# Experts taken one of each group in turn, and the way from the output projection to them rebuilt

## The reference, cut to what matters

```python
x = x + gate1 * (jnp.concatenate([gm_out, ssm_out], axis=-1) @ w_out[l])
h = rmsnorm(x, norm2_g[l]) * (1 + scale2) + shift2
x = x + gate2 * hier_moe(h, ...)          # then one final rmsnorm

def hier_moe(t, ...):
    g_prob = softmax(t @ w_rg + b_rg)               # 4 groups, the best one is taken
    e_logits = (t @ w_re + b_re).reshape(-1, 4, 4)  # 4 experts in each, the best two of the group
    gates = ...                                     # 16 weights per token, two of them not zero
    hid = silu(t @ w_gate[e]) * (t @ w_up[e]) * gates[:, e]     # 2048 -> 512
    out = sum over e of hid @ w_down[e]                         # 512 -> 2048
```

## Time and profile before

| | |
|---|---|
| three runs | 1430.35 (median), 1426.56, 4198.51 us |
| the profiled execution | 1430.36 us, of which its span is 1428.3 us |
| PE busy | 1198.2 us (84%) |
| PEld, DVE, ACT, POOL busy | 643.5, 310.4, 200.8, 116.0 us |
| chain that ended last | PE 65%, DMA 26%, DVE 6%, issue 1%, ACT 1% |
| L1163 (full branch, gate and up) | x256, 64 for each of four experts |
| L1160 (few branch, gate and up) | x1536, 128 for each of twelve experts |
| DMA moved | 401.09 MB, 281 GB/s in the mean |

### The profile page before, as it was taken

How to read it: one execution, slowest core, us unless ns; L and a number is a source line. 1 busy time by engine, 2 the same in 40 slices (tenths; PEclk the granted TensorE clock), 3 DMA queues, 4 the chain that set the end, 5 groups by cost and what they waited for, 6 DMA issues and landing times.

```text
span 1428.3 us, 16027 instructions
## 1 busy us (share of the span) xinstructions
PE 1198.2 (84%) x6320; PEld 643.5 (45%) x6321; DVE 310.4 (22%) x623; ACT 200.8 (14%) x385; POOL 116.0 (8%) x129
## 2 busy tenths in 40 slices
PE   2678999999999999999992299999988788778740
PEld 0225565565545445545542244444544444444420
DVE  0101222131122224120018500111111211111128
ACT  2001111012021222100012100010111111111102
POOL 2010000000000002000005100000000000000016
PEclk8778999989999999999995599999999999999975
DMA  9997787737557529642530468877999999999953
GB/s 333 421 350 279 282 336 291 278 143 294 232 197 281 230 73 357 225 189 77 226 118 33 177 247 305 308 276 296 378 413 412 414 412 402 393 412 412 425 204 105
DMA packets 71717, 401.09 MB, mean 281 GB/s; under 512 B 6489, under 2 KB 6713, under 8 KB 39645
## 3 DMA queue, kind: packets, MB, share of 16 engines
q1 hardware_dynamic: 63216, 368.59, 66.0%
q0 software_dynamic: 6944, 23.99, 5.1%
q10 hardware_dynamic: 1520, 7.98, 1.4%
HBM read 394.85 MB, written 17.22 MB: 288 GB/s over the span
## 4 chain that ended last, share of the span: by engine, by line
PE 65%; DMA 26%; DVE 6%; issue 1%; ACT 1%; SPq 0%; POOLq 0%; DVEq 0%
DMA arena<-in_w_up_dram 20%; PE bank L817 20%; PE bank L896 10%; PE bank L1163 8%; PE bank L823 5%; DMA arena<-in_w_ada_dram 5%; PE bank L810 5%; PE bank L1160 5%; PE bank L1186 4%; PE bank L914 1%; PE bank L1183 1%; DMA arena<-expert_rows 1%; PE bank L840 1%; DVE arena L1480 1%; DVE arena L1481 1%
## 5 line engine op out<-in xcount | busy, mean ns | idle before, releaser
L817 PE MATMUL bank<-arena 128*128 128x512 f32 x640 | 286.0, 597 | 0.0
L1160 PE MATMUL bank<-arena 128*64 128x256 f32 x1536 | 185.8, 399 | 59.9 <-DMA arena<-in_w_gate_dram 32.6
L817 PEld LDWEIGHTS bank<-arena 128*128 128x128 f32 x640 | 117.9, 190 | 135.5 <-issue 134.4
L1160 PEld LDWEIGHTS bank<-arena 128*64 128x64 f32 x1536 | 112.5, 143 | 138.0 <-DMA arena<-in_w_gate_dram 44.8
L896 PE MATMUL bank<-arena 128*128 128x320 f32 x512 | 143.2, 440 | 3.8 <-DVE arena L1258 3.8
L810 PE MATMUL bank<-arena 128*32 128x512 f32 x768 | 101.4, 669 | 44.5 <-DMA arena<-in_w_ada_dram 32.7
L896 PEld LDWEIGHTS bank<-arena 128*128 128x128 f32 x512 | 97.9, 192 | 51.1 <-issue 7.8
L1163 PE MATMUL bank<-arena 128*128 128x512 f32 x256 | 113.5, 604 | 7.5 <-issue 7.5
L1183 PE MATMUL bank<-arena 128*64 128x512 f32 x384 | 85.0, 595 | 6.0 <-DVE arena L1629 6.0
L1626 DVE SCALAR_TENSOR_TENSOR arena<-bank,arena 128x512 f32<-128x512 f32 x16 | 12.0, 751 | 348.5 <-PE bank L1160 232.4
L1163 PEld LDWEIGHTS bank<-arena 128*128 128x128 f32 x256 | 49.5, 194 | 70.2 <-issue 70.2
(11 more groups left out here) (314 smaller groups left out, 856.8 us busy)
## 6 DMA issues: line engine op xcount, KB each, us to landing
arena<-in_w_ada_dram SPq DMA_DIRECT2D x48, 2048.0 KB, 14.9
arena<-in_w_gate_dram SPq DMA_DIRECT2D x32, 2048.0 KB, 26.3
arena<-in_w_up_dram SPq DMA_DIRECT2D x32, 2048.0 KB, 27.1
arena<-in_w_down_dram SPq DMA_DIRECT2D x32, 2048.0 KB, 26.2
arena<-in_w_in_dram SPq DMA_DIRECT2D x20, 2048.0 KB, 7.8
arena<-in_w_out_dram SPq DMA_DIRECT2D x8, 2048.0 KB, 8.8
arena<-mod_final POOLq DMA_DIRECT2D x6, 1024.0 KB, 11.8
arena<-expert_rows SPq DMA_DIRECT2D x8, 512.0 KB, 8.6
```

The lines of the kernel that those rows point to most:

```text
L817: last = mm(banks[j][:, :], lhsT=xT_[:, t, OFF[j]:OFF[j] + P], rhs=w, start=start, stop=stop)
L1160: last = mm(PB[bank][64 * h:64 * h + 64, 0:HALF], lhsT=XeT[:, t0 + t, 0:64], rhs=slots_w[slot][:, t, HALF * h:HALF * h + HALF], start=star ...
```

## The change

Three things change together.

First, the experts run one of each group in turn: place 4r + g of the order holds expert 4g + r. SP's loads follow nested loops over r and g, and the routing masks are written in the new order (`by_turn`), so every table behind them is in it too. 

Second, the norm rows keep their column order. The `by_t` permutation is gone, and the gate and up weights are loaded so that the four input rows of a piece lie together in each partition (8 KB pieces instead of 16 KB), as the down weights already were; the transposes of the gathered rows read every fourth column instead. DVE multiplies x1 with the scale in each quarter (`scaled`) and, once the factor is known, applies factor and shift with two instructions per tile (`shifted`); POOL's part of the norm and its clearing of Xe are gone, and ACT issues all stores, two per tile.

Third, the last quarter of the projection goes token tile by token tile, with a semaphore `outp_done` after each prompt tile, so that residual, squares, factor and rows of a tile follow while PE works on the next. The wait of a down weight load for `h2_stored[2]` falls away, and small buffers move to places that are cleared early.

```diff
             def expert(e, i):
-                    if isinstance(i, int) and s == W1:
-                        sp.wait_ge(h2_stored[2], 16)
-                        src = w[0, bass.ds(e, 1)].rearrange("e (p t) n -> p (e t) n", t=KT)[:, 8 * half:8 * half + 8, :]
-                        dst = slots_w[s]
+                        src = w[0, bass.ds(e, 1)].rearrange("e (a p b) n -> p (e a) (b n)", p=P, b=4)[:, 2 * half:2 * half + 2, :]
+                        dst = slots_four[s]
...
-            with sp.Fori(1, NE) as e:
-                expert(e, e)
+            with sp.Fori(1, 4) as g:
+                expert(4 * g, g)
+            with sp.Fori(1, 4) as r:
+                with sp.Fori(0, 4) as g:
+                    expert(4 * g + r, 4 * r + g)
...
-            pool.memset(arena[:, SA + 2048:MX], 0.0).then_inc(cleared, 1)
-            pool.tensor_tensor(o, o, by_t(a2b[0:DEC, 1, :]), ALU.mult).then_inc(h2_sample, 1)
-            pool.tensor_tensor(o, o, by_t(s2b[0:DEC, 1, :]), ALU.add).then_inc(h2_sample, 1)
-            pool.memset(Xe, 0.0).then_inc(cleared, 1)
+            pool.wait_ge(yT_out, 24)
+            for a, b in ((cT_off, cT_end), (cw_off, cw_end), (wdt_off, wdt_end)):
+                pool.memset(arena[:, a:b], 0.0).then_inc(cleared, 1)
...
+            def store_h2(j):
+                n = NT[j]
+                act.wait_ge(h2_ready, j + 1)
+                act.dma_start(h2_d[OFF[j]:OFF[j] + n, 0:ROW], h2_part[j][0][0:n]).then_inc(h2_stored[j], 16)
+                act.dma_start(h2_d[OFF[j]:OFF[j] + n, ROW:D], h2_part[j][1][0:n]).then_inc(h2_stored[j], 16)
...
+                x1_square(3, j)
+                act.wait_ge(var, j + 2)
+                act.activation(st[0:n, 20 + j:21 + j], st[0:n, 16 + j:17 + j], ACT.Sqrt).then_inc(std, 1)
+                x1T_copy(3, j)
+                if j < 2:
+                    store_h2(j)
             act.wait_ge(gexp_in, 1)
...
+            store_h2(2)
...
-                        last = tr(PB[2 + k][:, P * c:P * c + P], Xe[:, P * t:P * t + P], ident)
+                        a, b = 4 * P * (t // 4), t % 4
+                        last = tr(PB[2 + k][:, P * c:P * c + P], Xe[:, a + b:a + 4 * P:4], ident)
...
+            def scaled(q, j):
+                n, cols = NT[j], slice(N * q, N * q + N)
+                dst = h2_part[j][1][0:n] if q == 3 else h2_part[j][0][0:n, cols]
+                step(V.tensor_tensor(dst, x1[0:n, j, cols], a2b[0:n, STREAM[j], cols], ALU.mult))
...
+            def shifted(j):
+                n, b = NT[j], STREAM[j]
+                left, right = h2_part[j][0][0:n], h2_part[j][1][0:n]
+                V.scalar_tensor_tensor(left, left, col(24 + j, 1, n), s2b[0:n, b, 0:ROW], ALU.mult, ALU.add)
+                V.scalar_tensor_tensor(right, right, col(24 + j, 1, n), s2b[0:n, b, ROW:D], ALU.mult, ALU.add).then_inc(h2_ready, 1)
...
+            for j in range(2):
+                dve.wait_ge(outp_done, j + 1)
+                residual(3, j)
+                scaled(3, j)
+                rstd_of(j)
+                shifted(j)
+            dve.wait_ge(slot_used[W1], 16)
+            residual(3, 2)
+            scaled(3, 2)
+            rstd_of(2)
             dve.wait_ge(lgp, 12)
...
             payload(0)
+            shifted(2)
             dve.wait_ge(rankp, 1)
```

More of the change, by code:

```diff
@@ L195, in trunk @@
         rt = take(3, 8)
+        assert ptr[0] <= cT_end
+        ptr[0] = cw_off
+        pay = take(3, COLS, 4)
         rk = take(3, COLS)
@@ L753, in _ @@
-            act.wait_ge(var, 2)
-            act.activation(st[:, 6:9], st[:, 3:6], ACT.Sqrt).then_inc(std, 1)
-            act.wait_ge(slot_used[W1], 16)
-            act.wait_ge(rstd2, 1)
-            act.activation(by_t(h2p[2][0:DEC], out=True), by_t(x1[0:DEC, 2, :]), ACT.Copy, scale=st[0:DEC, 11:12]).then_inc(h2_sample, 1)
-            for j in range(2):
-                act.wait_ge(h2_ready, j + 1)
-                act.dma_start(h2_d[OFF[j]:OFF[j] + P, :], h2p[j]).then_inc(h2_stored[j], 16)
+            def store_h2(j):
[3 more added lines that the diff above has]
+                act.dma_start(h2_d[OFF[j]:OFF[j] + n, ROW:D], h2_part[j][1][0:n]).then_inc(h2_stored[j], 16)
@@ new lines, in _ @@
+            for q in range(3):
+                if q:
+                    for j in range(3):
+                        x1T_copy(q - 1, j)
+                for j in range(3):
+                    x1_square(q, j)
+            for j in range(3):
+                x1T_copy(2, j)
+            for j in range(3):
+                n = NT[j]
+                if j == 0:
+                    act.wait_ge(outp_read, 9)
+                x1_square(3, j)
[4 more added lines that the diff above has]
+                    store_h2(j)
@@ L1488, in _, with residual @@
             V.tensor_scalar(fold, iota, 63.5, -64.0, ALU.is_gt, ALU.mult)
-            step(V.memset(rk, -1.0))
+            V.memset(rk, -1.0)
             for k in range(3):
                 V.tensor_scalar(w4[:, k, :], iota[:, 0:4], -1.0, 4.0, ALU.mult, ALU.add)
+            def residual(q, j):
+                k, n = 3 * q + j, NT[j]
+                bank, cols = PB[4 * (q % 2) + j], slice(N * q, N * q + N)
+                if j < 2:
+                    last = V.tensor_tensor(tmp, bank[:, :], g1b[:, 0, cols], ALU.mult)
+                else:
+                    for h in range(2):
+                        r, c0 = slice(DEC * h, DEC * h + DEC), HALF * h
+                        last = V.tensor_tensor(tmp[0:n, c0:c0 + HALF], bank[r, 0:HALF], g1b[r, 1, N * q + c0:N * q + c0 + HALF], ALU.mult)
+                last.then_inc(outp_read, 1)
+                dve.wait_ge(outp_read, k + 1)
+                V.tensor_tensor(x1[0:n, j, cols], x1[0:n, j, cols], tmp[0:n], ALU.add).then_inc(x1_ready, 1)
+                dve.wait_ge(x1_ready, k + 1)
@@ new lines, in shifted @@
+            def shifted(j):
[3 more added lines that the diff above has]
+                V.scalar_tensor_tensor(right, right, col(24 + j, 1, n), s2b[0:n, b, ROW:D], ALU.mult, ALU.add).then_inc(h2_ready, 1)
+            dve.wait_ge(g1_in, 32)
+            dve.wait_ge(xr_in, 48)
+            for q, (slot, used) in enumerate(((A1, 21), (W1, 15), (A1, 22))):
+                dve.wait_ge(slot_used[slot], used)
+                for j in range(3):
+                    residual(q, j)
+                if q == 0:
+                    dve.wait_ge(s2_in, 64)
+                for j in range(3):
+                    scaled(q, j)
```

160 lines of the change are left out of this document (76 added, 84 removed).

## The result

The changed kernel takes **1374.8 us** in the median (1373.5 to 1376.2), the kernel before 1428.5 in the same comparison: a ratio of 0.961, 95% interval [0.958, 0.964]. The prediction was 1370 us with a range of 1354 to 1389. The ratio is of fast runs alone: one of the four of the kernel before, 4198.5 us, counts in its median and not in the ratio.

The account below looks back on a forecast made before the run. PE idles in the transition behind DVE's wide norm instructions; four full experts are PE bound, eleven DMA bound. 1428.3 - 34 - 27 + 0.5 = 1367.8 us of span, plus 2.1 around it: 1370 us, range 1354 to 1389.

Parts of the forecast that it names:

- the transition: From the projection's last matmul to the first expert's first: -27 us, bounds -21 and -28.
- -26.9 - 0.8 + 0.7 + 0.5: Up to the first expert's matmul: logits reduced earlier, POOL's clearing of Xe gone, `shifted(2)` before the ranks, strided transposes.
- the load layout: Gate and up weights in 8 KB pieces instead of 16 KB: taken as 0 us.
- Faster loads: Rival in the experts' stage: all loads run at 422 GB/s rather than 408, 15 us gained, 1355 us; chance 0.11.
- the order of the experts: Experts' stage: three later full experts cost 32.4 us instead of 44.7; -34 us, bounds 28 and 37.
- I take 1 us each: Experts' stage: extra cost of each later full expert, which gathers and scatters more rows; 0.6 us worked out, 1 taken.
- 27 us of queued loads against 12.3 us of lag: Experts' stage: a full expert puts PE 12.3 us behind; 27 us of queued loads do not run empty.
- The loads do not run through a full expert: Rival in the experts' stage: DMA engines pause at each full expert as before, 1404 us; chance 0.06.
- Half the transition comes back: Rival: PE stalls in the last quarter or the store before the gather, 1383 us; chance 0.11, shared with late gathers.
- The loads lose rate: Rival in the experts' stage: smaller pieces load slower; chance 0.03 for no or little gain, 0.03 for slower.

Follow-up runs that it names:

- quarter_whole: The changed kernel with the last projection quarter's tiles in the old order, both prompt tiles at once; 1375.5 us, ratio 0.962 to the kernel before.
- rest_only: The changed kernel with the experts in the old order (0 to 15), keeping the rebuilt transition and load layout; 1401.2 us, ratio 0.980 to the kernel before.
- pieces16: The changed kernel with gate and up weights in 16 KB pieces again and transposes at every 16th column; 1371.6 us, ratio 0.959 to the kernel before.
- order_only: The kernel before with the new order of the experts alone; 1400.4 us, ratio 0.981 to the kernel before.
- pairs: The changed kernel with two experts of each group in turn, full ones at places 0, 1, 8, 9; 1387.6 us, ratio 0.971 to the kernel before.

## Why the prediction was right, point by point

**Right: which stages, and by what.** The forecast was that the transition loses DVE's wide instructions and that a full expert among short ones costs the loads' time and not TensorE's. Both hold by the runs that do one alone.

**Right in size: the transition.** -26.9 - 0.8 + 0.7 + 0.5 = -26.5 were predicted up to the first matmul, -27.7 measured. The 0.5, for the strided transposes at place 0, did not show: they took 3.69 us against 3.68. The parts agree too: the last quarter 42.0 us (predicted 39.2 + 2.9 = 42.1), the logits 4.2 us behind it (4.5), `shifted(2)` 1.81 + 0.74 on the way to the ranks (2.5), the gather as late after the ranks as before. Within it the prediction named the tile order and the wide instructions together; `quarter_whole` shows that the former carries about 2 us.

**Right: nothing from the load layout.** `rest_only` leaves the stage at 551.8 us against 550.7, `pieces16` is the same as the changed kernel. "Faster loads" (1355) did not happen: the stage moved by 2 us at most with the layout.

**Mis-sized: the order of the experts.** -34 were predicted and -26.9 measured (-28.3 in `order_only`), on either side of the term's lower bound, 28. The step that failed is "I take 1 us each" for what a full expert costs the DMA engines beyond a short one. Four places take 132.4 us in the mean; with three short ones at 32.4 the full one takes 35.2, which is 2.8 more, not 1. About 1 us is its rows: before, the queue of the indirect gathers and scatters moved 2.71 MB in three full experts (870 to 1004 us),

```profile
q0 software_dynamic: 736, 2.71, 5.6%
```

and 3.59 MB in seven short ones (1069 to 1301),

```profile
q0 software_dynamic: 1568, 3.59, 4.8%
```

that is 0.90 MB against 0.51, and 0.39 MB at 408 GB/s are 1.0 us. The other 1.7 are the pause around the down part, shown above as 1.7, 2.7 and 1.6 us at the three places: the prediction held 27 us of queued loads against 12.3 us of lag, but buffers come free by pairs, with 10 us between the second up load and the first down load. Nor was the lag 12.3 at places 4 and 8: those experts took 46.9 us (928.53 to 975.41, 1060.67 to 1107.56), and only that at place 12 took 45.2. Taking 1.8 us too little at each of three places explains 5.4 of the 7.1 us; the rest, under 2 us, was not followed further.

**The rivals.** "The loads do not run through a full expert" is out by the shares at places 4, 8 and 12: what is left of it is the pauses of about 2 us, and the second of each pair in `pairs`. "Half the transition comes back" is out: PE is busy 41.97 of 42.00 us in the last quarter. "The loads lose rate" is out: 404 and 410 GB/s over a full expert and over 48 us, with the smaller pieces. The Trainium skill (DMA: Bandwidth & Descriptors, Where 436 GB/s comes from) states that about 358 GB/s per core binds transfers between HBM and SBUF; these rows disagree, so the rule does not hold for this kernel.

**What would show it.** Logits within 6 us of the last matmul (4.2), first matmul near 796 (796.7), the full branch at 0, 4, 8 and 12, a share of at least 0.95 over places 4 and 8 as a whole (not over each 3 us of them), and no wait for `h_rows` behind place 0: all as named. The period of 33.1 us per place is just above the 32 to 33 named, and that small excess is the term's error.

## What to carry to other kernels

Where two kinds of work are bound by different engines, mix them in turn, and check that the buffered loads cover the lag of one long item: here one was carried at a cost of 2.8 us, the second of a pair no more. Begin with a short item, since its buffers are the first that come free (8 to 12 us here). The order suits this input, whose four full experts are all of group 0; no run has another. Before splitting elementwise work between DVE and POOL, look in the trace at what each instruction then costs: here both grew, and giving it all to DVE was faster.

## What the runs showed of the hardware that was not expected

- The first expert through TensorE's loop stood 6.3 us when its code was the second branch (7.9 us from the transposes to the first matmul against 2.0, and its first matmuls 30.72 us at a granted clock of 0.90 against 27.76 at 1.00); later experts switched branches without a stall. Before and after pay this alike, so it is no part of the difference. A late block of the instruction queue fits, as said above; the cause is not shown.
- Weight loads of transposes at a step of 16 bytes took 213 ns, more than at 64 bytes (196), against 141 for neighbouring columns. The Trainium skill (SBUF — State Buffer, SBUF: two separate sides and its note on cachelines) states that a step of four float32 is free; the rows disagree. It cost nothing here, even at place 0, where no weights are awaited: its 16 transposes took 3.69 us against 3.68 before.
- After a wait of some 30 us for weights, the full experts at places 4 and 8 took 29.46 us for their 64 matmul instructions, at a granted clock of 0.94 over them (1.0 is the upper level, 2.4 GHz). That at place 12, after a wait as long, ran at 1.00 and took 27.76; those that follow one another without a wait in `rest_only` took 27.50. What decides between the two after a wait is open.
